# A conditioning stage with one buffer per weight group and two chains of squares, and a last value tile that starts with the latent columns

## The reference, cut to what matters

```python
sh1, sc1, g1, sh2, sc2, g2 = adaln(c, ada_w, ada_b)       # silu(c) @ ada_w + ada_b, also for c_ctx
h_lat = modulate(rms_norm(x, norm_mix_g), sh1, sc1)        # h * (1 + scale) + shift
h_ctx = modulate(rms_norm(x_ctx, norm_mix_g), csh1, csc1)
p = concatenate([h_ctx, h_lat]) @ w_in                     # q, k, v, a, b, ...
qkv = silu(short_conv(qkv))                                # 5 taps, context and latents apart
q, k = l2_normalize(q), l2_normalize(k)
```

## Time and profile before

| | us |
|---|---|
| median of 3 runs | 4622.8 (4618.36 to 4623.26) |
| the profiled execution, its own time | 4621.78 |
| its span in the profile | 4620.0 |
| conditioning, to the last `mod` | 63.9 |
| start of the first big product | 87.5 |
| end of the last product of v | 334.9 |
| first product of the scan | 361.4 |

### The profile page before, as it was taken

One profiled execution on the slowest core, in us unless ns is written; L12 is line 12 of the kernel. 1 busy time (PEld: TensorE's weight loads), 2 busy tenths in 40 slices (PEclk: granted clock), 3 DMA queues, 4 the chain that ended last, 5 costly groups with the idle time before them and its releaser, 6 DMA issues.

```text
span 4620.0 us, 46359 instructions
## 1 busy us (share of the span) xinstructions
PE 4249.3 (92%) x18566; PEld 3097.0 (67%) x18566; DVE 2177.3 (47%) x3670; ACT 1573.8 (34%) x3044; POOL 900.7 (19%) x695
## 2 busy tenths in 40 slices
PE   7886889988999999988889999899989898999997
PEld 3446754757788888645457866565665677888886
DVE  2368844123556663336262327572655744333334
ACT  3566741132211111332332215353545633222222
POOL 2112225211434441016161000011000021000002
PEclk9998899999999999898979999999999999999999
DMA  5112242111334431311111210111000031111111
GB/s 196 51 58 92 82 150 87 28 64 64 105 105 116 117 114 48 109 56 46 55 46 55 78 45 22 34 63 54 14 23 19 19 128 32 51 46 55 46 39 62
DMA packets 257799, 308.89 MB, mean 67 GB/s; under 512 B 19072, under 2 KB 209936, under 8 KB 256304
## 3 DMA queue, kind: packets, MB, share of 16 engines
q1 hardware_dynamic: 238096, 227.15, 15.8%
q0 software_dynamic: 17408, 75.64, 5.2%
q10 hardware_dynamic: 2080, 3.15, 0.2%
HBM read 271.61 MB, written 34.28 MB: 66 GB/s over the span
## 4 chain that ended last, share of the span: by engine, by line
PE 63%; DVE 9%; ACT 5%; POOL 2%; issue 1%; DMA 0%; POOLq 0%; DVEq 0%; ACTq 0%
PE bank L194 61%; PE bank L197 2%; DVE Mx L214 1%; ACT at21P L203 1%; ACT at20P L203 1%; ACT Mx L203 1%; POOL sq L214 1%; DVE at21sm L232 1%; DVE at20sm L232 1%; DVE x L220 1%; DVE wfl L214 0%; DVE at20Pl L214 0%; DVE at21Pl L214 0%; DVE at11sm L232 0%; DVE at10sm L232 0%
## 5 line engine op out<-in xcount | busy, mean ns | idle before, releaser
L194 PE MATMUL bank<-h,wslot 128*128 128x512 f32 (+2 forms) x1616 | 682.9, 560 | 13.9 <-ACT h L203 3.8
L194 PE MATMUL bank<-hT,wslot 128*128 128x512 f32 (+3 forms) x1136 | 461.0, 562 | 13.9 <-DMA hT<-hspill 6.6
L194 PEld LDWEIGHTS bank<-h,wslot 128*128 128x128 f32 (+1 forms) x1616 | 288.1, 189 | 241.7 <-issue 225.6
L194 PEld LDWEIGHTS bank<-hT,wslot 128*128 128x128 f32 (+1 forms) x1136 | 211.7, 189 | 238.8 <-issue 232.3
L194 PE MATMUL bank<-ffn1h,wfh 128*128 128x512 f32 x704 | 279.8, 397 | 11.8 <-DVE ffn1l L220 10.9
L194 PE MATMUL bank<-ffn2h,wgh 128*128 128x512 f32 x704 | 276.3, 392 | 9.9 <-DVE ffn2l L220 9.5
L220 DVE SCALAR_TENSOR_TENSOR x<-bank,mod,x 128x512 f32<-128x512 f32 x224 | 164.3, 746 | 245.9 <-PE bank L194 245.4
L194 PE MATMUL bank<-ffn1l,wfh 128*128 128x512 f32 x704 | 274.9, 391 | 0.0
L194 PE MATMUL bank<-ffn2l,wgh 128*128 128x512 f32 x704 | 274.7, 390 | 0.0
L194 PE MATMUL bank<-ffn2h,wgl 128*128 128x512 f32 x704 | 274.6, 390 | 0.0
L194 PE MATMUL bank<-ffn1h,wfl 128*128 128x512 f32 x704 | 274.5, 390 | 0.0
(11 more groups left out here) (565 smaller groups left out, 9297.9 us busy)
## 6 DMA issues: line engine op xcount, KB each, us to landing
wslot<-in_w_in SPq DMA_DIRECT2D x40, 1024.0 KB, 5.5
ffn1t<-in_w_mod POOLq DMA_DIRECT2D x64, 512.0 KB, 4.8
wslot<-in_w_ffn_in SPq DMA_DIRECT2D x44, 512.0 KB, 5.2
Mx<-acsT SPq DMA_DIRECT2D x32, 512.0 KB, 4.8
at1w<-in_ada_w POOLq DMA_DIRECT2D x24, 512.0 KB, 4.7
wslot<-in_ffn_w_gate SPq DMA_DIRECT2D x22, 512.0 KB, 3.9
wslot<-in_ffn_w_up SPq DMA_DIRECT2D x22, 512.0 KB, 5.2
wslot<-in_w_ffn_out SPq DMA_DIRECT2D x20, 512.0 KB, 5.3
```

Of the source, the lines that this page charges most:

```text
L194: return Counted() if counting[0] else self.q.matmul(o, l, r, start=start, stop=stop)
```

## The change

Weights of the conditioning get 8 buffers of their own, so that all their loads are issued at once. The constants and parameters come in two parts each, the second part behind the conditioning's weights. The first product's weights (`ab`, and group 2 of `w_in`) are issued at the end of `a_sp`. All three ranges of the input are issued by ACT.

The sum of range 0 stands ahead of group 0, those of ranges 1 and 2 ahead of groups 3 and 4. The squares of range 2 go through a ring of their own and are added on DVE. ACT squares ranges 1 and 2 in turns. The multiplication by the root (`unit`) is taken out of the modulation, and stands before the gains are known: on DVE for range 0 and 5 tiles of range 1, on POOL for 3 tiles of range 1 and all 8 of range 2. What is left when the gains come is one instruction for each tile: on DVE for even tiles, on ACT for odd ones.

The last value tile (`m` 11) takes the ranges as latents, latents, context. Its taps, silu and transposes go in two parts, 260 to 1284 and 0 to 256, and its `more(3)` goes. The loads `kks` of the scan's first two steps move from behind the end of `gp` to ahead of that tile's `vspill`, behind the last product.

```diff
     class Ada:
         def sp(self, e, g):
-            load(e, (self.nm, g), [(self.w, 0, 8, g * 256, 256, 0)])
+            e.dma_start(self.bufs[g][:, :]..., self.w[:, g * 256:(g + 1) * 256]...).then_inc(self.w_in[g]("in"), 16)
...
     class NormMod:
+        def unit(self, e, part, n0, n, ks):
+            e.wait_ge(*self.rs(n0))
+            for k in ks:
+                e.tensor_tensor(self.h(k, n0, n), self.x(k, n0, n), self.rstd[:, n0:n0 + n], OP.mult)...
+        def dve(self, e, i):
+            for k in range(0, 8, 2):
+                e.tensor_scalar(a, a, gs[...], self.shift(k, w), OP.mult, OP.add)...
+        def act(self, e, i):
+            for k in range(1, 8, 2):
+                e.activation(a, a, AF.Identity, scale=self.gs[...], bias=self.shift(k, w))...
...
     def a_sp(e):
-        e.dma_start(cst[:, :], io["cst"])
-        e.dma_start(par[:, :], io["par"])
-        x_load(e, 1)
+        e.dma_start(par[:, 0:PAR0], ...)
+        e.dma_start(cst[:, 0:CST0], ...)
         for g in range(8):
             ad1.sp(e, g)
+        load(e, ("ab",), [(w1, 0, 8, 2048, 16, 0)])
+        e.dma_start(par[:, PAR0:pn], ...)
+        load(e, ("qkv", 2), [(w1, 0, 8, 512, 256, 0)])
+        e.dma_start(cst[:, CST0:cn], ...)
     def a_pe(e):
+        rms1.sum_pe(e, *ALL[0])
         for g in range(9):
-            if g in DUE:
-                rms1.sum_pe(e, *ALL[DUE[g]])
+            if g == 3:
+                rms1.sum_pe(e, *ALL[1])
+            if g == 4:
+                rms2.sum_pe(e, *ALL[2])
             ad1.pe(e, g)
     def a_act(e):
+        for i in range(3):
+            x_load(e, i)
         ad1.act(e)
         e.ln_exp_table()
+        rms1.square(e, *ALL[0])
+        rms1.root(e, *ALL[0])
+        rms1.square(e, *ALL[1], range(4))
+        e.wait_ge(*xa_in[2].after("in"))
+        for j in range(4):
+            rms1.square(e, *ALL[1], [4 + j])
+            rms2.square(e, *ALL[2], [2 * j, 2 * j + 1])
+        rms1.root(e, *ALL[1])
+        rms2.root(e, *ALL[2])
     def a_dve(e):
+        nm1.unit(e, n1.dve, *ALL[0], range(8))
+        ad1.dve(e, 0)
+        rms2.adds(e, range(1, 4))
+        ad1.dve(e, 1)
+        rms2.adds(e, range(4, 8))
+        for g in range(2, 5):
+            ad1.dve(e, g)
+        nm1.unit(e, n1.dve, *ALL[1], range(5))
+        for g in range(5, 9):
+            ad1.dve(e, g)
     def a_pool(e):
+        rms1.adds(e)
+        nm1.unit(e, n1.pool, *ALL[1], range(5, 8))
+        nm1.unit(e, n1.pool, *ALL[2], range(8))
...
+    QKV = [(i, m, ALL[1:] if m < 4 else ALL[1:] + ALL[:1] if m == LAST else ALL) for i, m in enumerate(SEQ)]
+    def v_runs(m):
+        return ((2, 4), (6, 4), (0, 2)) if m == LAST else ((0, 2), (2, 4), (6, 4))
+    def conv_parts(m):
+        return [(260, 1284), (0, 256)] if m == LAST else [(260 if m < 4 else 0, 1284)]
     def gp_sp(e):
         for m in range(8, 12):
+            if m == LAST:
+                e.wait_ge(*gp.pe.after("mm", m, 0))
+                e.wait_ge(*hs_out.after("out"))
+                kks(e, 0)
+                kks(e, 1)
     def gp_dve(e):
-            if i > 8:
+            if i > 8 and m != LAST:
                 more(3)
```

More of the change, by code:

```diff
@@ L302, in build @@
     bank = [ctx.enter_context(nc.psum_tensor(f"bank{i}", [128, 512], f32)) for i in range(8)]
-    cst_in, par_in, out_sem = Sem("cst", 16), Sem("par", 16), Sem("out", 16)
+    cst_in, par_in = [Sem(f"cst{i}", 16) for i in range(2)], [Sem(f"par{i}", 16) for i in range(2)]
+    out_sem = Sem("out", 16)
     def C(n, a=0, b=None):
@@ L472, in squares, with square @@
                 self.square(e, n0, n)
[L474 to L477, removed]
+        def square(self, e, n0, n, ks=range(8)):
+            for k in ks:
+                sq = self.ring.take(self.nm, n0, k)
+                for ev in self.ring.freed(self.nm, n0, k):
                     e.wait_ge(*ev)
@@ L517, in __init__ @@
             self.mv, self.scj, self.shj, self.gname, self.rstd, self.gs, self.rs = mv, scj, shj, gname, rstd, gs, rs
-        def dve(self, e):
+            self.units = {(n0, k): st.pool if i == 2 or (i == 1 and k >= 5) else st.dve for i, (n0, n) in enumerate(rngs) for k in range(8)}
+        def unit(self, e, part, n0, n, ks):
+            e.wait_ge(*self.rs(n0))
+            for k in ks:
+                e.tensor_tensor(self.h(k, n0, n), self.x(k, n0, n), self.rstd[:, n0:n0 + n], OP.mult).then_inc(part(self.nm, "u", n0, k), 1)
@@ L649, in a_pool @@
         for n0, n in ALL:
-            e.wait_ge(*nm1.ready(n0))
+            for ev in nm1.ready(n0):
+                e.wait_ge(*ev)
         e.dma_start(io["hspill"], hT[:, :]).then_inc(hs_out("out"), 16)
-    w1 = io["w_in"]
     m2 = mark("right")
@@ L861, in gates_in_place, with kks @@
                                 OP.mult).then_inc(gs.dve(*(("gn", B) if i == len(runs) - 1 else ("gn", B, i))), 1)
+    def kks(e, s):
+        for d in range(2):
+            c = order[d][s]
+            if s >= 2:
+                e.wait_ge(*gs.pe.after("pt", s - 2, d))
+            e.dma_start(kkE[s % 2][d][:, :], io["kks"][c * 128:(c + 1) * 128, :]).then_inc(kk_in[s % 2](s, d), 16)
     def gp_sp(e):
-        load(e, ("ab",), [(w1, 0, 8, 2048, 16, 0)])
-        for g in (2, 3, 0, 1):
+        for g in (3, 0, 1):
             load(e, ("qkv", g), [(w1, 0, 8, g * 256, 256, 0)])
@@ L944, in v_tokens @@
                     e.wait_ge(*ev)
-                e.wait_ge(*gp.act.after("silu", m))
+                e.wait_ge(*gp.act.after("silu", m, part_of(m, c0)))
                 for x in range(nn):
@@ L1023, in k_tokens, with tap_act @@
                 bk_p.give(("kt", c), gp.act.now())
+        def tap_act(m, raw, p):
+            a, b = conv_parts(m)[p]
+            acc = accs.take("acc", m)
+            for ev in accs.freed("acc", m):
+                e.wait_ge(*ev)
+            e.wait_ge(*gp.act.after("raw", m, 768))
+            e.activation(acc[:, a:b], raw[:, a:b], AF.Copy, scale=par[:, cw + m:cw + m + 1]).then_inc(gp.act("tap", m, p), 1)
+            return acc
         for i, m, rngs in QKV:
@@ L1210, in gs_sp @@
             e.wait_ge(*ev)
-        def kks(s):
-            for d in range(2):
-                c = order[d][s]
-                if s >= 2:
-                    e.wait_ge(*gs.pe.after("pt", s - 2, d))
-                e.dma_start(kkE[s % 2][d][:, :], io["kks"][c * 128:(c + 1) * 128, :]).then_inc(kk_in[s % 2](s, d), 16)
         def chunk(s):
@@ L1226, in chunk @@
                 e.dma_start(vb[d][:, :], io["vspill"][c * 128:(c + 1) * 128, :]).then_inc(vb_in[d](s), 16)
-        for i in range(2):
-            e.wait_ge(*kk_out[i].after(8 + i))
-        kks(0)
-        kks(1)
         for d in range(2):
```

186 lines of the change are left out of this document (103 added, 83 removed).

## The result

The changed kernel takes 4609.3 us (median of 15 runs, 4605.5 to 4613.1), the kernel before 4622.9 beside it (15 runs, 4618.0 to 4628.6). The ratio is 0.9972, 95% interval 0.9964 to 0.9980: **faster by 13.6 us**, 9 to 17 by the interval. The forecast was 4607.5, between 4600 and 4615, with 0.86 on faster.

What follows compares the result with a forecast made beforehand. PE was taken as the bound, with only its idle or slow time in the first 375 us removable: 4621.8 - 8.2 (front) - 7.0 (tail) = 4606.6, given as 4607.5 us for the median, 8 in 10 between 4600 and 4615.

Steps and rivals of the forecast that it cites:

- The bound: Whole kernel: PE is busy 92% of the span, so only its idle or slow time in the first 375 us can go.
- Part 1: Data arrival at the start: input ranges at about 10, 18 and 27 us, all weights by 42, well ahead of PE.
- the weights take the rest: groups 0 and 1 at about 12 and 20: Conditioning's loads: weights use bandwidth the input leaves; group 2 at 27, then 3 us each, the last at 42.
- range 0 shares evenly: First input load: half of 341 GB/s beside the weights, 1.05 MB at 0.175 MB/us, there at about 10 us.
- The rival of a late last range: Input loads: ACT's queue gets half the bytes, not packets; last range 5 us later, total 4612.5; chance 0.14.
- Part 2: Conditioning's squares and PE's start: range 1's sum at 35.5, gains at 59.0, 5.0 us earlier.
- The rival built on it: DVE's queue between copies of rows 0 to 5: DVE and POOL exclude each other, 27 us, total 4632; chance 0.05.
- Part 3: Modulation up to the first big product: gains of 2.2 and 1.0 us, product at about 79.3, 8.2 earlier in all.
- Parts 4 and 5: Last value tile and scan's start: copies end 2.7 us earlier, loads no longer awaited, POOL next late; 7.0 together.
- the 7.0: Gain in us taken for the last value tile and the scan's start together, bounds 2.7 and 8.5.
- the rival falls in which a new wait takes their place: Scan's start: POOL's masks or `vb` hold the scan, only the copies' 2.7 us pass, total 4611.8; chance 0.11.
- The sum: Whole kernel: 4621.8 - 8.2 - 7.0 = 4606.6 us for the profiled execution, given as 4607.5 for the median.

Runs made afterwards that it cites:

- the last experiment: Changed kernel with range 2 issued behind the first root, squares by range, range 2's additions behind row 2, its sum before group 5, later units on POOL: 4610.0 us.
- the experiment: Changed kernel with the loads of `kkE` back behind the end of the stage, all else kept: 4612.7 us, ratio 0.9977 to the kernel before.
- the tail alone: Kernel before with only the changes of the last value tile and the earlier `kkE` loads: 4619.7 us, ratio 0.9993.
- the conditioning alone: Changed kernel with the last value tile's order and the `kkE` loads as before, run twice: 4617.5 and 4617.8 us, ratios 0.9989 and 0.9983.

## Why the prediction was right, and where it was not

**The bound.** Right: PE has the same work, the gain lies in the first 375 us and is carried through; no stage behind `vn` changed by over 2 us in this pair (first to last `vn` 213.3 before, 211.4 after; from there to `wfh` 555.2 and 555.0; from there to the end 3477.0 and 3476.6). But this sign is weak. Over the 14 profiles of this case, whose program is the same there, the three stages lie between 211.1 and 214.9, 551.7 and 556.8, and 3474.0 and 3481.3. Two profiles that agree to 0.4 us at the end do so by luck, and "over 2 us" would have told nothing.

**Part 1.** The sharing by packets and the rate of the 2 KB queue were right, the order was not. The step that failed is "the weights take the rest: groups 0 and 1 at about 12 and 20", and ahead of it "range 0 shares evenly": the weights had hardly begun at 6 us, and 700 packets of the input stood against 56 in the 2 us ahead of that. Range 0 landed 6.2 us after its issue, at 7 instead of 10, so the 2 KB packets came into play sooner, and the weights had 0.125 MB/us from 6 us on. Group 0 came at 15.50 and group 1 at 23.85, where PE stood 0.40 and 3.62 us. It cost little, for sum 1 at 33.69 was what PE would have had to wait for otherwise. The rival of a late last range fell by the same rows: it came at 24, before the forecast's 27.

**Part 2.** Sum 1 stood at 33.69 instead of 35.5, since range 2 was early; the prediction's own sign of 35 to 37 missed it. From there the sum of the prediction gives 57.2 for the gains; they came at 58.29. The 1.1 us between are the wait of 1.15 behind DVE's five units, which it put "at nothing", naming their cover. That cover was one group of 4.08 us; the units took 8.27, a little above the 8 named as their bound, and row 5 was late. The Trainium skill, SBUF — State Buffer, "Who interferes with whom", says that a two-input DVE instruction and a reading GpSimd instruction lock each other out for a whole instruction. The runs agree: 0.68 us alone became 1.65 beside POOL, and POOL's 1.26 became 1.71; in the last experiment 0.24 became 3.64. The rival built on it, 27 us on PE's path, did not come. It needed 0.9 us for each of the 20 instructions. In the trace of after 12 of the 20 took visibly longer than alone: three of range 0's units (1.48 instead of 0.42), four additions (0.83 to 1.58 instead of 0.68) and the five units of range 1 (1.58 to 1.75). That is 11 us, 0.9 for each meeting but 0.56 for each of the 20, and PE waited for 1.15 of it. The prediction's 12 meetings were the right count; its cover failed in one place.

**Part 3.** From the gains to the first `ab` product 2.41 us (forecast 2.1), PE idle 2.65 (2.4). The clock held its upper level through these products in this profile: 17.3 us to the first big product instead of the forecast's 18.2 (19.2 less 1.0). In the other profiles with this front it is 17.3 to 20.1: 17.3 where the clock stays up, 18.9 to 19.0 with 3.4 us at the lower level, 19.9 to 20.1 with 5.4 to 5.7. The forecast's middle value was fair, and this profile lies at its good end.

**Parts 4 and 5.** Here the prediction named its own mark, "wrong if `vn` moves by less than 5 against the big products". It moved by 4.3 (286.98 to 282.70), so **by its own mark the 7.0 was too much**. The mechanism was right: no DMA in front of the product, POOL next. The terms that were mis-sized are three. The copies moved by 1.6 against the first big product, not 2.7: the taps began 0.3 us later than forecast and took 7.31 us for 6.9, and the transposition, forecast to fall into a wait, took 1.94 us in DVE's row between the taps and the copies, so that these ended 3.5 us behind the taps and not 3.0. POOL's first `Dm` and `DT` took 2.06 and 1.98, not 1.5 each, beside DVE's product with `kkE`, which is once more two-input work against POOL: 1.0 us. And PE's 8 products took 2.04, where 8 of the same shape took 1.16 in the earlier trace rows: 0.9 us, at a clock of 0.50 against 1.00 in the two windows above, and the prediction had no term for it. The loads' own share, 3 to 4 by the experiment against 4.3, was about right, and with it the rival falls in which a new wait takes their place: `vn` moved 2.7 more than the copies did. Other pairs of profiles give other numbers for the same edits: 3.5 between the kernel before and the tail alone, 7.5 between the conditioning alone and after. From the first big product to `vn` the clock is at its lower level for 10.2 us less in the pair that gives 7.5, and for 6.8 less in those that give 4.3 and 3.5. So part of what the tail wins may be clock, and how much is open.

**The sum.** A front of 9.6 in place of 8.2 and a tail of 4.3 in place of 7.0 were followed by 2.5 us more in and behind the scan, 1.9 of them from the first to the last `vn`, which lies within the scatter given above. Against the medians, 13.6 us were won where the sum had 15.2. That the time came within 2 us of the forecast is in part luck: the front gave 1.4 us more and the tail 2.7 less. The split by whole runs, 4.9 to 6.7 for the conditioning, about 4.8 for the last tile without the loads (from 4617.5 to 4612.7 in one set), 2.3 to 3 for the loads, is good to some 3 us in each term. What stays open is why the clock stays low longer with the conditioning alone, and with it some of its gain is given back at the scan's start.

**What in the change works.** In the front, as the table is read: PE's start, 7 us earlier, from a small first part of the constants and range 0 alone at the head of ACT's queue; sums that PE reaches without waiting; and the units ahead of the gains, which leave 2.4 us of modulation in place of 4.3. Not the eight buffers, and not the two chains, as far as 3 us of noise let one see. That an early start or the units ahead of the gains is the larger of these was argued from the table, and not tried by itself. In the tail: the loads, and 1 to 2 us that either of two edits would bring.

## What to carry to other kernels

A saving on the engine that bounds a stage is only as good as the work that the next step needs from a shared port: look for two-input DVE instructions beside a stream of POOL work, small ones too, and keep the ones on the critical path out of that company. Where loads from two queues meet, work out their shares by packets and not by bytes, and do not let a computing engine issue more than about two and a half thousand rows ahead of work that it must do soon. When a change has several parts, measure them one by one: here two of five (a buffer per group, the second chain) cost effort and brought nothing that could be measured.

## What was not expected of the hardware

- **Large loads in a row hold the engine that issues them.** ACT issued three loads in 3.08 us, but five loads of 1024 rows of 1 KB took 14.24, and ACT computed nothing until 15.08, with some 2560 rows still under way. SP's eight loads of the same size took 31.33 us after; on SP nothing else was waiting.
- **A tiny instruction can wait for several large ones.** One DVE instruction on a 128x8 tile, 0.17 us in another run, took 3.57 while POOL ran its units back to back at 1.25 each: nearly three of them. DVE's five units, against the same kind of work, took turns with POOL's one by one. What decides between the two is not shown.
- **The clock scatters between profiles of like kernels.** The same 17.3 us of `ab` products became 18.9 or 19.9 with 3.4 or 5.4 us at the 1.2 GHz level, and the end of the program, from the first product with `wfh` on, scattered by 7 us over 14 profiles. A profile's end can so move by some us with no cause in the code.
